# Attention stages without copied operands, and one meeting of the engines per border between stages

## The reference

```python
# first block: 8 query heads share 2 key heads of 64, window of 128 to both sides, a sink per head
scores = einsum('bnqhgd,bnkhd->bnhgqk', qb, kb) * (64 ** -0.5)      # 128 queries x 384 keys
scores = where(valid, scores, -inf)
mx = maximum(max(scores, -1), sink); p = exp(scores - mx)
out = einsum('bnhgqk,bnkhd->bnqhgd', p / (sum(p, -1) + exp(sink - mx)), vb)
# second block: 8 heads of 64 with keys of their own, chunks of 64 queries, 8 chunks to the left
scores = einsum('bcqhd,bckhd->bhcqk', qc, kb) * scale + bias         # 64 queries x 576 keys
p = softmax(where(kpos >= 0, scores, NEG_BIG)); out = einsum('bhcqk,bckhd->bcqhd', p, vb)
```

## Time and profile before

| what | us |
|---|---|
| median of three executions | 3396.28 |
| the profiled execution, its own time | 3399.98 |
| its span, first to last instruction | 3398.2 |
| wa, from the meeting before to the meeting behind | 1291.9 to 1487.1 |
| ca, the same | 2720.3 to 2994.8 |
| PE busy, share of the span | 3078.1 (91%) |
| DVE, ACT, POOL busy | 1824.4, 1279.3, 603.7 |
| mean granted TensorE clock | 0.945 of full speed |

### The profile page before, as it was taken

The page is one execution under the profiler, slowest core; times in us unless marked ns, Lnnn a source line. Parts: engine busy times, 40 slices in busy tenths (PEclk is TensorE's granted clock), DMA queues, the critical chain, the costliest instruction groups (busy, mean ns, idle before and its releaser), DMA issues. The chain is left out here.

```text
span 3398.2 us, 61959 instructions
## 1 busy us (share of the span) xinstructions
PE 3078.1 (91%) x23542; PEld 2561.5 (75%) x23542; DVE 1824.4 (54%) x3251; ACT 1279.3 (38%) x2654; POOL 603.7 (18%) x539
## 2 busy tenths in 40 slices
PE   5998998796999998969939999999999979979799
PEld 4886997686999995648838888878888746658687
DVE  5555443073555644655475577575676456643433
ACT  4222333152444445851052323342323357730132
POOL 0000000052233330123203233242232111100000
PEclk7999999896999998979969999999999979989899
DMA  4211764253333333125463312353222261154443
GB/s 131 73 68 64 250 232 164 76 156 110 117 121 125 132 123 112 62 92 195 170 211 113 105 66 81 109 186 107 92 69 101 92 194 50 31 186 173 179 148 117
DMA packets 289608, 423.26 MB, mean 125 GB/s; under 512 B 41568, under 2 KB 178784, under 8 KB 284256
## 3 DMA queue, kind: packets, MB, share of 16 engines
q1 hardware_dynamic: 238784, 379.68, 33.2%
q10 hardware_dynamic: 50592, 40.38, 3.8%
HBM read 270.56 MB, written 149.42 MB: 124 GB/s over the span
## 5 line engine op out<-in xcount | busy, mean ns | idle before, releaser
L106 PE MATMUL pj_pp<-h_hi,pj_whi 128*128 128x512 f32 x1152 | 450.4, 391 | 5.4 <-POOL h_lo L2916 5.4
L108 PE MATMUL pj_pp<-h_hi,pj_wlo 128*128 128x512 f32 x1152 | 449.2, 390 | 0.0
L107 PE MATMUL pj_pp<-h_lo,pj_whi 128*128 128x512 f32 x1152 | 449.2, 390 | 0.0
L106 PEld LDWEIGHTS pj_pp<-h_hi,pj_whi 128*128 128x128 f32 x1152 | 216.7, 188 | 51.1 <-issue 6.6
L108 PEld LDWEIGHTS pj_pp<-h_hi,pj_wlo 128*128 128x128 f32 x1152 | 216.6, 188 | 45.0
L107 PEld LDWEIGHTS pj_pp<-h_lo,pj_whi 128*128 128x128 f32 x1152 | 216.8, 188 | 44.7
L2743 ACT CAST pj_whi<-w_raw 128x512 fp32r<-128x512 f32 x192 | 119.2, 622 | 326.7 <-PE pj_pp L108 315.0
L2807 DVE TENSOR_TENSOR pj_wlo<-w_raw,pj_whi 128x512 fp32r<-128x512 f32 x192 | 160.4, 836 | 13.4 <-ACT pj_whi L2743 10.4
L106 PE MATMUL pc_pp<-h_hi,pc_whi 128*128 128x512 f32 x384 | 150.8, 393 | 10.3 <-DVE pc_wlo L346 10.3
L1075 DVE COPY_PREDICATED ds_z<-ds_zmask,ds_ps 128x128 f32<-128x128 int32 x160 | 47.2, 301 | 194.0 <-PE ds_ps L1304 194.0
L108 PE MATMUL pc_pp<-h_hi,pc_wlo 128*128 128x512 f32 x384 | 150.5, 392 | 0.0
(11 more groups left out here) (351 smaller groups left out, 7695.8 us busy)
## 6 DMA issues: line engine op xcount, KB each, us to landing
w_raw<-in_w_second SPq DMA_DIRECT2D x192, 256.0 KB, 2.8
ds_pk<-scratch_pack SPq DMA_DIRECT2D x32, 1280.0 KB, 7.8
scratch_pack<-rp_out SPq DMA_DIRECT2D x32, 512.0 KB, 2.7
scratch_sig_fm<-pj_ob SPq DMA_DIRECT2D x64, 256.0 KB, 2.1
mb_sg<-scratch_sig_fm SPq DMA_DIRECT2D x16, 1024.0 KB, 7.8
rp_fm<-scratch_qkv_fm SPq DMA_DIRECT2D x96, 128.0 KB, 2.8
scratch_qkv_fm<-pc_acc SPq DMA_DIRECT2D x11, 1024.0 KB, 4.8
n_x<-in_x SPq DMA_DIRECT2D x16, 512.0 KB, 4.1
```

Of the source, the lines that this page charges most:

```text
L106: nc.tensor.matmul(out, ah, bh, start=(first and i == 0), stop=False)
L107: nc.tensor.matmul(out, ah, bl, start=False, stop=False)
L108: mm = nc.tensor.matmul(out, al, bh, start=False, stop=(last and i == n - 1))
```

## The change

Two edits that touch all stages, and one that rewrites `attention`.

A stage no longer clears its semaphores when it ends; the list USED holds them, and the next stage's `open_block`, after its own semaphores have been allocated and given START, lets POOL clear them. The second meeting is gone from the 12 borders; after the last stage the clear and a meeting are still there. SP adds no START any more: POOL has two turns in five.

In `attention` the tiles `q`, `k` and `v`, the copies, the semaphores for them, POOL's whole program and the two counters `waited` and `pool_waited` are gone. PE reads `qr`, `kr` and `vr`, and waits for `tile_in` itself. All 16 tiles are written out, so every address and count is a constant.

```diff
+USED = []
 class Ctx:
     def __exit__(self, *e):
         r = self.stack.__exit__(*e)
         if e[0] is None:
-            self.nc.clear_and_free_semaphores(self.used)
-            self.nc.all_engine_barrier()
+            self.last.extend(self.used)
         return r
+    def open_block(self):
+        if self.last:
+            self.nc.clear_and_free_semaphores(self.last)
+            self.last.clear()
+        return self.stack.enter_context(self.nc.Block())
...
-        engines = (self.nc.gpsimd, self.nc.scalar, self.nc.vector, self.nc.tensor, self.nc.sync)
+        engines = (self.nc.gpsimd, self.nc.scalar, self.nc.vector, self.nc.tensor, self.nc.gpsimd)
...
-    with Ctx(nc, name) as c:
+    with Ctx(nc, name, USED) as c:
...
-        q = [c.sb(f"q{s}", [P, nq, P]) for s in S]
-        k = [c.sb(f"k{s}", [P, nk_tiles, n_kt * P]) for s in S]
-        v = [c.sb(f"v{s}", [P, n_kt, vw]) for s in S]
...
-        block = c.stack.enter_context(nc.Block())
+        bias_in = c.sems("bias_in", PAIRS)
+        block = c.open_block()
...
-        def program(eng, tile, flush=None):
-            for t in range(first):
-                tile(fixed(t - 1) if t else None, fixed(t), fixed(t + 1))
-            with eng.Fori(0, (end - first) // 2) as j:
-                for t in (first, first + 1):
-                    tile(in_loop(j, t - 1), in_loop(j, t), in_loop(j, t + 1))
-            for t in range(end, TILES):
-                tile(fixed(t - 1), fixed(t), fixed(t + 1) if t + 1 < TILES else None)
-            if flush:
-                flush(fixed(TILES - 1))
+        def program(tile, flush):
+            for t in range(TILES):
+                tile(span_of(t - 1) if t else None, span_of(t))
+            flush(span_of(TILES - 1))
...
-        @block.gpsimd
-        def _(pool):
-            def tile(before, now, after):
-                t, u, s, lo, n, b0 = now
-                tile_loaded(pool, t)
-                for g in G:
-                    wait(pool, weighed[g], PAIRS * (t - 1))
-                pool.sem_inc(pool_waited, 1)
-                nc.gpsimd.tensor_copy(q[s][:], qr[:, :, bass.ds(t * P, P)]).then_inc(qv_staged[s], 1)
-                nc.gpsimd.tensor_copy(v[s][:, 0:n, :], vr[:, bass.ds(lo, n), :]).then_inc(qv_staged[s], 1)
-            program(pool, tile)
...
                 if m == 0:
-                    pe.wait_ge(qv_staged[s], 2 * u + 2 + START)
-                    pe.wait_ge(k_staged[s], u * nk_tiles + nk_tiles + START)
+                    pe.wait_ge(tile_in, LD * 16 * min(TILES, t + ahead + 1) + START)
...
-                        mm = nc.tensor.matmul(s_ps[g][:, a:a + w], q[s][rows, m, :], k[s][rows, key_tile(m), a:a + w],
-                                              start=True, stop=True)
+                        mm = nc.tensor.matmul(s_ps[g][:, a:a + w], qr[rows, m, t * P:(t + 1) * P],
+                                              kr[rows, key_tile(m), lo * P + a:lo * P + a + w], start=True, stop=True)
...
-                        mm = nc.tensor.matmul(o_ps[half][HD * g:HD * g + HD, m % 2, :], v[s][:, a, v0:v0 + HD],
+                        mm = nc.tensor.matmul(o_ps[half][HD * g:HD * g + HD, m % 2, :], vr[:, lo + a, v0:v0 + HD],
...
-            def stage_k(now, a):
-                t, u, s, lo, n, b0 = now
-                if a == 0:
-                    tile_loaded(dve, t)
-                nc.vector.tensor_copy(k[s][:, a, 0:n * P], kr[:, a, bass.ds(lo * P, n * P)]).then_inc(k_staged[s], 1)
...
-                        dve.sem_inc(waited, 1)
...
-                        if after and 4 <= h < 4 + nk_tiles:
-                            stage_k(after, h - 4)
...
-            for a in range(nk_tiles):
-                stage_k(fixed(0), a)
...
+    nc.clear_and_free_semaphores(USED)
+    USED.clear()
+    nc.all_engine_barrier()
```

More of the change, by code:

```diff
@@ L263, in project_conv @@
     LAST = DN_TILES - 1
-    with Ctx(nc, "pc") as c:
+    with Ctx(nc, "pc", USED) as c:
         raw, whi, wlo = weight_tiles(c)
@@ L399, in rows_prepare @@
     C2 = 2 * P
-    with Ctx(nc, "rp") as c:
+    with Ctx(nc, "rp", USED) as c:
         S = range(2)
@@ L682, in gate_rows_decays @@
     N = TILES * GATES
-    with Ctx(nc, "pg") as c:
+    with Ctx(nc, "pg", USED) as c:
         raw = c.sb("wraw", [P, KT, WIDTH])
@@ L863, in delta_scan @@
     cols = [slice(h * P, (h + 1) * P) for h in range(4)]
-    with Ctx(nc, "ds") as c:
+    with Ctx(nc, "ds", USED) as c:
         ident = c.sb("ident", [P, P])
@@ L1450, in gates_rope @@
     PAIRS = TILES // 2
-    with Ctx(nc, "gr") as c:
+    with Ctx(nc, "gr", USED) as c:
         S = range(2)
@@ L1814, in attention, with span_of @@
         bias_parts = 1 if sinks else PAIRS
-        bias_in = c.sems("bias_in", PAIRS)
         LD = load_tile.n_dma
         def wait(eng, sem, count):
-            if not (isinstance(count, int) and count <= 0):
+            if count > 0:
                 eng.wait_ge(sem, count + START)
-        def fixed(t):
+        def span_of(t):
             lo = max(0, t + ahead + 1 - n_kt)
@@ L1950, in behind, with tile @@
                     spread(t2, m2 // 2)
-            def tile(before, now, after):
+            def tile(before, now):
                 for m in range(PAIRS):
@@ L2057, in _ @@
                 dve.wait_ge(bias_in[0], 16 + START)
-            program(dve, tile, flush)
+            program(tile, flush)
         @block.scalar
@@ L2095, in store, with tile @@
                 act.wait_ge(normed[s], u + 1 + START)
-                act.dma_start(out[:, :, bass.ds(t * P, P)].rearrange("m p t -> p m t"), ob[s][:]).then_inc(
+                act.dma_start(out[:, :, t * P:(t + 1) * P].rearrange("m p t -> p m t"), ob[s][:]).then_inc(
                     stored[s], 16)
-            def tile(before, now, after):
+            def tile(before, now):
                 for m in range(PAIRS):
@@ L2128, in flush @@
                 store(last)
-            program(act, tile, flush)
+            program(tile, flush)
 def mix_output(nc, consts, delta_o, norm_row, sw_fm, gate_rows, gate_fm, raw, x, out):
     W = DN_W
-    with Ctx(nc, "mo") as c:
+    with Ctx(nc, "mo", USED) as c:
         S = range(2)
@@ L2560, in shapes @@
         return count(("z", "sig", "mix") if b in (C12, C22) else ("z", "sig"), u)
-    with Ctx(nc, "pj") as c:
+    with Ctx(nc, "pj", USED) as c:
         S = range(2)
@@ L2989, in merge_branches @@
     K4 = 4
-    with Ctx(nc, "mb") as c:
+    with Ctx(nc, "mb", USED) as c:
         S = range(2)
@@ L3142, in final_output @@
 def final_output(nc, m_fm, w_out, x, norm_row, out):
-    with Ctx(nc, "fo") as c:
+    with Ctx(nc, "fo", USED) as c:
         S = range(2)
```

27 lines of the change are left out of this document (8 added, 19 removed).

## The result

| | before | changed |
|---|---|---|
| median, first measurement (10 runs each) | 3403.74 us | 3370.76 us |
| ratio, with its interval | | 0.9902 [0.9881, 0.9922] |
| median, second measurement (20 and 6 runs) | 3404.68 us | 3360.88 us |
| ratio, with its interval | | 0.9863 [0.9837, 0.9890] |
| profiled execution: own time / span | 3399.98 / 3398.2 us | 3362.23 / 3360.3 us |

A forecast was written before the change was run, and what follows sets the result against it. PE, busy in 91% of the span, was taken as the bound, with gains from its idle time. Borders 13.9, ca 13.8 and wa 3.0 sum to 30.7 us: 3396.28 to 3365.6 us, own range 3358 to 3374, with rivals 3354 to 3380.

The forecast's parts named there:

- What bounds: Whole kernel: PE is busy in 91% of the span, so gains must come from its idle time at borders and attentions.
- Borders, forecast 13.9: 12 borders: SP's first load follows the meeting without second meeting or additions; 13.2 us in eleven stages plus 0.7 in pj.
- Rival 2: Borders: only the second meeting is gained, 8.4 us, as first loads then wait for something else; 3371 to 3372 us, chance 9%.
- POOL behind its additions: Stage starts: POOL adds more START and clears, so its first pj product comes some 0.8 us later; cost taken as 0.
- ca, forecast 13.8: ca: 11.9 us from PE's idle time at 14 tile starts, 1.5 in tile 0, 0.4 in tiles 2 and 3.
- rival 1: ca: another wait, PE for ScalarE, takes over behind the copies; two thirds of ca's gain lost, 3375 us, chance 13%.
- tile 0: Start of ca: without copies behind head 4, tile 1's scores start earlier; 1.5 us taken, bounds 0 and 2.4.
- wa, forecast 3.0: wa: PE starts 1.2 us earlier without POOL's copies, 1.0 from key copies over 14 tiles, 0.8 from loop turns.
- Loop turns, forecast 0.8 in wa and 0 in ca: Attention loops: 5 turns in wa cost PE 0.16 us each; in ca written-out and looped tile starts look alike.
- Instructions late: Attentions: 22 more written-out tiles must be fetched, up to 2.8 us each, 62 us lost, 3427 us; chance 4%.
- The clock: Start of ca: the low-clock stretch moves with the work, possibly ending up to 3 us of work later or earlier; 1.5 us either way.
- rival 3: Behind the borders: low-clock stretches get shorter as idle time before them does; 10 us more gained, 3355 us, chance 11%.

The follow-up runs named there:

- borders alone: Kernel before with only the new borders (one meeting, later clear by POOL, no START on SP), attentions still looping and copying; ratio 0.9944 to the kernel before.
- two kernels with the old borders: Kernel before with only the new attentions, ratio 0.9930; kernel before with its attention tiles written out, copies kept, ratio 0.9967.
- with zeros: Changed kernel plus 5 to 48 PE products of a zero tile between meeting and each stage's first product; ratio 0.9847 to the kernel before, median 3352.25 us.
- the last kernel: Changed kernel plus zero products in longer counts, ca's first bias part ahead of tile 0, one early exp on ScalarE; ratio 0.9849, 3350.09 us.

## Why the prediction was right, and where its terms were off

- **What bounds: right.** Nearly the whole gain is PE's idle time, at the two places that were named.
- **Borders, forecast 13.9.** SP's path was read right, and so was that nearly all of it arrives: 15.6 us less on SP, and with the borders alone 13.3 less up to PE's first products. In the changed kernel, outside the attentions, PE's first products come 9.4 us earlier over ten borders, against 10.4 forecast (9.7 in nine and 0.7 in pj; pj measured 0.6). Alone the borders gave 19 us (12 to 26). Rival 2 (the second meeting only, 8.4) falls: the run that removes just that brings PE's first products 7.9 us earlier, and the additions give the other 5.4.
- **POOL behind its additions, forecast 0.8 us later in pj, cost 0.** Its first work there came 3.1 us behind the meeting, where it was 1.9: 1.2 later, and nothing was late for it.
- **ca, forecast 13.8, with its border 15.5; measured 17.8 and 17.4.** The mechanism was right: idle before the scores gone, nothing took its place, which is rival 1 refuted. Two terms were mis-sized. The larger is ca's start: PE's first product comes 3.4 and 3.2 us earlier (in the two profiles of the changed kernel), where the sum has 1.7 for the border and nothing for the copies ahead of tile 0. The border alone gave 2.1, and POOL's copies, put back, cost 0.8 to 1.0; the sum had such a term in wa (1.2) and left it out in ca. The other is the tile: 0.95 us instead of 0.87. The sum took PE's labelled idle time; the distance from the start of the last transposes to that of the scores was the better measure, and went from 1.25 to 0.31 us. From the first tile's start to the last one's ca is 14.9 and 14.4 us shorter, forecast 13.8: tile 0 gave 1.7 and 0.5 (forecast 1.5), tiles 1 to 4 in the first profile 0.0, 1.7, 1.2 and 0.95. That the whole tile term was the key copies' is only partly so: with the loop and VectorE's counter already gone they were worth 0.60 us. The change took the loop and the counter away together with the copies, so the sum didn't have to tell them apart; whether it would have come out with either kept wasn't run, and luck may be part of it.
- **wa, forecast 3.0, with its border 4.8; measured 5.8 and 7.4.** The first product comes 2.9 and 3.1 us earlier, forecast 3.0. The rest gives 2.9 us instead of 1.8 in the first profile: two tiles 0.40, not 0.30, and tile 1 another 0.5.
- **Loop turns, forecast 0.8 in wa and 0 in ca.** This term was wrong in ca. I had compared a written-out tile's start with one in the loop (0.89 and 0.87) and found them alike; but the first is that of a shorter tile. Written out, the same tile lost 0.15 us. The Trainium skill's rule (Runtime: NRT & Kernel Launch, Instruction fetch mechanics), that a taken branch out of the fetched pages has to wait for a fetch, would by the prediction's estimate have made 24 us of the turns. The two attentions lost 4.6 us by being written out, and the packets of the instruction queue speak against a fetch at each turn, so by these runs its effect is small here.
- **Instructions late: refuted.** 22 more tiles of code brought 17 more packets in q8, 0.27 MB, and no gap in PE.
- **The clock, forecast as 1.5 us either way, and a rival of 10 us at 11%.** It may have been too small. The time at the lower clock, ds left out, is 319 us before and 296 and 281 in the changed kernel. At half speed that would be, as an estimate, up to 11 and 19 us, the size of what the sum left unexplained. But two kernels with the old borders show 297 and 300 as well, so the effect of the change is not set apart from the scatter, and rival 3 stays open. What the runs do show is that the low clock behind the borders depends on what PE did ahead of it: 211 us with zeros. That it costs time shows in wa (3.7 to 5.3 us); over the whole kernel the span less ds is 8 us below the mean of the two changed ones, which is within scatter, and the ratio's interval lies below that of the first measurement only.
- **project_second.** 3.3 and 4.0 us less where 0.7 was forecast. The excess can't be put down to the change: borders alone show 0.4 less there, and the kernel before with its attentions written out, whose project_second and borders are those of before, 3.2 less.

The stages' differences add to 38 us in the first pair of profiles, against 30.7: ca and wa 3.3 more than forecast, project_second 2.6, the rest in other stages' scatter. Open is how much of the second measurement's 47 us is chance; its interval reaches down to 37.

## What to carry to other kernels

Where an engine waits at the turn of a tile, look which instruction was the last to end before it starts, and ask whether the data could be read where it lies: here waiting for key copies, the last of them 0.49 us long and at the end of the engine's queue, cost 0.6 us of every ca tile, while the same copies unread cost a tile nothing. Look for bookkeeping on the same chain too: an addition to a counter ahead of a maximum delayed it by 0.18 us. At a border, what the loading engine does before its first load is nearly all on the path, instruction by instruction (12.6 of 13.7 us in eleven stages). And when a stage's start is slow, read the granted clock before counting instructions.

## What was not expected of the hardware

- Extra meetings of all five engines mostly took 0.33 us each on SP (39 of them, 14.2 us together); the drain and clear between the two old meetings made up the rest of 0.7.
- Zeros on PE brought the clock up before the real work: in the kernel with zeros, products of 128 x 512 came every 0.43 us at first and every 0.22 us by their end, at 11 of the 12 borders (project_second, with the fewest, stayed at 0.43).
- The clock fell in ca a second time without a long idle gap of PE: in the last kernel it went to half at 2706.3, with no more than 0.8 us of idle at once since the zeros, while PE did small products.
- One addition to a semaphore by VectorE, 0.05 us long in the trace, put off the maximum behind it by 0.18 us.
- delta_scan, the same instructions each time, took 505.9 us with 40 us at the lower clock and 522.3 with 83.
